# Prefill attention of a decoder layer: the products with a value block move from the middle of each step to its end

## The reference

```python
logit_own = jnp.einsum('hqd,hkd->hqk', q_c, k_own, ...) * scale + rb_t[:, t5_bucket(dist_own)]
...
p = jax.nn.softmax(logits, axis=-1)
...
out = jnp.einsum('hqnk,hqnkd->hqd', p_sel, v_sel) + jnp.einsum('hqk,hkd->hqd', p_own, v_own)
```

## Time and profile before

| | |
|---|---|
| runs, us | 1364.17, 1362.61, 1364.41 (median 1364.17) |
| profiled execution, us | 1363.37 |
| its span, first to last instruction, us | 1361.7 |
| TensorE busy | 1222.3 us, 90% |
| VectorE, ScalarE, GpSimd busy | 28%, 17%, 14% |
| mean granted TensorE clock | 0.967 of full speed |

### The profile page before, as it was taken

One profiled execution on the slowest core, in us unless ns is written; L12 is line 12 of the kernel. 1 busy time (PEld: TensorE's weight loads), 2 busy tenths in 40 slices (PEclk: granted clock), 3 DMA queues, 4 the chain that ended last, 5 costly groups with the idle time before them and its releaser, 6 DMA issues.

```text
span 1361.7 us, 17800 instructions
## 1 busy us (share of the span) xinstructions
PE 1222.3 (90%) x6825; PEld 693.6 (51%) x6825; DVE 383.8 (28%) x764; ACT 235.1 (17%) x514; POOL 189.7 (14%) x282
## 2 busy tenths in 40 slices
PE   4989988999999999999999997998887888778986
PEld 2344443485757676788888455333333333233432
DVE  3478975513323233100000226211001001100104
ACT  4122234322323232100000122000000000000002
POOL 2422333101111111100000001010101000110000
PEclk9999998999999999999999997999989999989998
DMA  9988999962827242651105516999999999999965
GB/s 356 347 248 294 368 387 363 372 249 62 336 71 240 63 120 55 178 143 63 62 0 222 195 31 195 367 406 423 423 424 424 427 423 422 426 421 424 424 290 201
DMA packets 116152, 372.59 MB, mean 274 GB/s; under 512 B 10948, under 2 KB 56533, under 8 KB 96622
## 3 DMA queue, kind: packets, MB, share of 16 engines
q1 hardware_dynamic: 93664, 308.96, 58.9%
q0 software_dynamic: 19280, 55.49, 12.1%
q10 hardware_dynamic: 3134, 7.16, 1.5%
HBM read 359.29 MB, written 22.36 MB: 280 GB/s over the span
## 4 chain that ended last, share of the span: by engine, by line
PE 67%; DMA 23%; DVE 4%; ACT 2%; SPq 1%; issue 1%; POOL 0%; ACTq 0%; POOLq 0%; DVEq 0%
PE ps L1683 64%; DMA ring<-in_w_exp_up 20%; PE ps L1694 3%; DMA ring<-in_cache_k 2%; DMA work<-in_x_prompt 1%; DVE ring L1156 1%; SPq L452 1%; DVE work L1378 1%; DMA hx<-expert_rows 1%; SPq L476 0%; ACT hx L697 0%; DVE work L1672 0%; SPq L450 0%; DVE work L1677 0%; DVE work L1639 0%
## 5 line engine op out<-in xcount | busy, mean ns | idle before, releaser
L1683 PE MATMUL ps<-ring,work 128*64 128x512 f32 (+3 forms) x1952 | 449.3, 598 | 68.7 <-DMA ring<-in_w_exp_up 47.6
L1683 PEld LDWEIGHTS ps<-ring,work 128*64 128x64 f32 (+2 forms) x1952 | 160.9, 144 | 321.7 <-issue 268.7
L1683 PE MATMUL ps<-ring,hx 128*32 128x256 f32 (+3 forms) x1584 | 272.7, 444 | 9.7 <-ACT hx L720 4.1
L1683 PEld LDWEIGHTS ps<-ring,hx 128*32 128x32 f32 (+1 forms) x1584 | 159.0, 146 | 106.1 <-issue 84.8
L1683 PE MATMUL ps<-hx,ring 128*128 128x272 f32 x768 | 179.1, 393 | 0.6 <-DVE work L1378 0.6
L1683 PEld LDWEIGHTS ps<-hx,ring 128*128 128x128 f32 x768 | 145.2, 190 | 31.2 <-DVE work L1378 1.1
L1683 PE MATMUL ps<-work,ring 128*128 128x272 f32 (+2 forms) x464 | 97.7, 369 | 0.7 <-ACT ring L988 0.7
L1637 DVE TENSOR_TENSOR work<-work,ps 128x256 f32<-128x256 f32 x32 | 13.5, 421 | 280.1 <-ACT work L1026 280.1
L1694 PE MATMUL ps<-cst,work 128*128 128x128 f32 (+4 forms) x349 | 65.9, 308 | 28.1 <-DVE work L1263 7.7
L1683 PEld LDWEIGHTS ps<-work,ring 128*128 128x128 f32 (+1 forms) x464 | 81.4, 188 | 18.6 <-issue 2.7
L1026 ACT ACTIVATE work<-ps 128x256 f32<-128x256 f32 x32 | 12.3, 384 | 434.7 <-PE ps L1683 434.7
(11 more groups left out here) (306 smaller groups left out, 762.0 us busy)
## 6 DMA issues: line engine op xcount, KB each, us to landing
ring<-in_w_exp_down SPq DMA_DIRECT2D x32, 2048.0 KB, 22.5
ring<-in_w_exp_gate SPq DMA_DIRECT2D x31, 2048.0 KB, 17.7
ring<-in_w_exp_up SPq DMA_DIRECT2D x31, 2048.0 KB, 22.2
ring<-in_w_ada SPq DMA_DIRECT2D x12, 2048.0 KB, 22.2
ring<-in_cache_k SPq DMA_DIRECT2D x64, 256.0 KB, 6.0
ring<-in_cache_k POOLq DMA_DIRECT2D x64, 256.0 KB, 5.9
ring<-in_cache_v SPq DMA_DIRECT2D x64, 256.0 KB, 8.7
ring<-in_cache_v POOLq DMA_DIRECT2D x64, 256.0 KB, 6.2
```

Source lines behind the costliest of these rows:

```text
L1683: return pe.matmul(out, lhsT, rhs, start=start, stop=stop, **k)
```

## The change

In each step of the loop on TensorE the value block is issued last, behind the turns of unit z-2 and the products with v of unit z-3, where it stood ahead of both.

```diff
                 if z == SELECT_AT:
                     selected(0)
-                if z <= PAGES:
-                    page_values(z - 1)
                 if 2 <= z <= UNITS + 1:
                     y = z - 2
...
                     last.then_inc(s("p_pv"), 1)
+                if z <= PAGES:
+                    page_values(z - 1)
             for half in range(2):
                 for k in range(KD):
```

## The result

The changed kernel took 1367.43 us (median of 13 runs, 1365.29 to 1369.73), the kernel before 1363.84 us (13 runs, 1361.71 to 1365.11). The ratio is 1.0027, with a 95% interval of 1.0019 to 1.0035: slower by 3.6 us, give or take 1.1. The forecast was 1367.8 us and +3.6 us.

The account below looks back on a forecast made before the run. The prediction took TensorE's issue order to bound the stage in steps 4 to 18: 4.35 us of waits added less 0.76 given back, net +3.6 us on 1364.17, gives 1367.8 us. Range for 8 in 10: 1364.8 to 1369.9 us.

Parts of the forecast that it names:

- No load bounds the stage: Steps 4 to 18: TensorE's issue order bounds the stage, value blocks are never waited for; later loads cost 0.
- The waits of steps 12 and 16: Turns of units 10 and 14 wait for ScalarE's copy behind long units' scores: +1.50 and +1.92 us.
- the cover theory: Experiments' theory: the loss is the value block no longer ahead of turns following long units' scores, in steps 8, 12, 16.
- The wait of step 8: Turns of unit 6 wait for the copy of unit 5: +0.48 us, after 0.10 already waited in step 7.
- Steps 6 and 7: Products with v wait for ScalarE's line 778, whose copy ran under the value block: +0.35 and +0.10 us.
- Given back: Block 8's wait for VectorE's line 1251 goes, -0.45 us; the wait before unit 15's turns goes, -0.31 us.
- The sum: Whole stage: 4.35 us added, 0.76 us given back, net +3.6 us, giving 1367.8 us.
- The clock: Rival: TensorE's clock falls in the new waits of 1.50 and 1.92 us, giving 1369.6 or 1371.4 us; chance 0.13.
- a drop of the clock near 266 us: Sign in the changed kernel's trace that would show the prediction wrong, as would a drop near 248 us.
- The start-up: Step 3's wait grows from 0.38 to 2.3 us, covered before step 4's turn; work after 208.79: 0, some tenths either way.
- Passed on in full: Behind the stage, TensorE's progress releases everything, the experts' loads too, so all 3.6 us reach the end.
- The rival of a shift taken up in the experts' stage: Experts' loads running ahead absorb the 3.6 us: 1364.2 us, or up to 1366.9 if in part; chance 0.21.

Follow-up runs that it names:

- The two kernels with early blocks: Kernel before, value blocks 3 and 4 run ahead of step 4's turn: 1362.38 us, 0.9995; with step 9's block at the end too: 1363.04 us, 0.9997.
- Both kernels that undo or isolate these steps: Changed kernel, block back in the middle in steps 8, 12, 16: 1363.46 us, 1.0000; block at the end in steps 12, 16 only: 1367.97 us, 1.0030.
- the second profile: The changed kernel profiled once more, nothing altered: one execution of 1363.49 us, stage 69.07 us, from step 5 62.81 us.
- changed, wait filled: Changed kernel plus three products that nothing reads, inside the wait of step 16: 1367.01 us, ratio 1.0024 to the kernel before.
- end in 16 only: Kernel before with the value block at the end in step 16 alone: 1364.78 us, ratio 1.0010.
- end in 9 only, chain sooner: Kernel before with the block at the end in step 9 alone, and ScalarE's copy and VectorE's normalisation sooner: 1363.00 us, ratio 0.9993.

## Why the prediction was right

- **No load bounds the stage.** Right for this change: no value block waits for a load in the changed kernel. The last load of a value block was issued at 253.36 us and took 11.2 us, so landed at 264.6 (forecast 263.8); block 15 ran at 269.48. The two kernels with early blocks show how near the loads are.
- **The waits of steps 12 and 16.** Forecast +1.50 and +1.92, measured 1.45 and 1.86 us. Both kernels that undo or isolate these steps move the time as the cover theory has it, and the two that move ScalarE's copy, or copy and normalisation, up in their queues take these waits away or shrink them to 0.44 us, so the cause is shown.
- **The wait of step 8.** Forecast +0.48, measured 0.38.
- **Steps 6 and 7.** Forecast +0.35 and +0.10, measured 0.56 and 0.34: the mechanism right, the terms too small. I allowed 0.04 us from the end of a copy to TensorE's start; behind line 778 it is 0.14 us (the copy of step 6 ends at 222.25, the products start at 222.39). And a turn that follows another turn starts 0.49 us after it (215.99 to 216.48) where the value block started 0.58 us after it (215.09 to 215.67), so TensorE arrives sooner and waits longer, at no cost.
- **Given back.** -0.45 and -0.31, both as forecast; the 0.48 us for line 1263 stayed, as forecast.
- **The sum.** The brackets add 4.59 and give back 0.76: 3.8 us. Of that some 0.3 us (the difference to the times from step 5) is TensorE's earlier arrival, above all in steps 5 to 7, and the time from step 5 is 3.5 us longer in the second profile, and in the first less its fall, against 3.6 in the forecast. The whole stage of the first profile is 6.10 us longer than before and that of the second 3.47; between the two lie 1.7 us of clock in step 16 and 0.95 us behind the cold start. That the median moved by 3.6 us too, to the tenth, is luck: its interval reaches from 2.6 to 4.8 us.
- **The clock.** I gave it 0.13 as a rival. It did fall behind the wait of step 16 in the profiled execution, and cost 1.70 us in one block (3.62 less 1.92); a drop of the clock near 266 us stood among the signs of being wrong, and this one came, at about 269.6. The waits alone, 3.5 us, account for the median; whether falls add to it is open. The Trainium skill ("TensorE: Matmul & The Clock Gate", section "HAM oscillation — how this bites in real kernels") describes a kernel in which every wait for a load, each longer than the new waits here, throttles the engine anew. The trace before agrees for its wait of 7.73 us. For waits as short as these the section has no case, and the traces are divided: a fall behind the 1.86 us of step 16 in two of four, and none at the 1.45 us of step 12, where the clock read 1.00 from 245 to 252 us in all four traces that have that wait.
- **The start-up.** The 2.24 us of idle time in step 3 was taken up, as forecast, by the idle time ahead of the turn of step 4, which VectorE still ends and which shrank from 7.73 to 5.88 us. The work of step 4, from its turn to that of step 5, was put at "some tenths either way". Single executions differ by more: 6.30 us before, 7.21 and 6.26 changed. But the order shows no price in it: it took 5.88 to 6.86 us in the five traces with the block in the middle there, and 5.65 to 7.21 in the six with it at the end.
- **Passed on in full.** From the gate rows to the end it is 1087.5 and 1087.2 us in the two profiles of the changed kernel, against 1087.3. The rival of a shift taken up in the experts' stage would have needed up to 3.6 us less there, and has fallen.

## What to carry to other kernels

When an independent piece of work is moved within a software-pipelined loop, count how many such pieces stand between each producer on the bound engine and its consumer one step on; here a price came only at the interval that shrank, and nearly all of it in the steps where the chain through the other engines is longest. Its size can be read off beforehand: the time at which the releasing instruction ended, less the time at which the moved piece used to start. If the other engines' queues can be reordered to fit, the price may vanish without touching the bound engine.

## What was not expected of the hardware

The granted clock is not a function of the order alone: with the same instructions and an idle time of 1.86 or 1.87 us ahead, the next value block took 3.62 us in one execution and 1.92 us in another, and the block behind the cold start 3.30 and 2.35 us. Nor is a short wait safe because it is short. In three of the thirteen traces ("changed, wait filled", "end in 16 only", "end in 9 only, chain sooner") the clock fell behind the wait of 1.01 us ahead of the gate rows, a wait that all thirteen have, and cost about 1.6 us. With the two at step 16 these are five falls behind short waits. In all five the clock still read 1.00 through the wait, and fell 0.6 to 1.5 us after TensorE had started again (an estimate from the means of windows of 1 us); what decides is not shown.

And 4 us of spread between runs, more than this change moves, come in part from before the stage: the same instruction began at 205.49 us in one execution of the changed kernel and at 208.78 us in another.
